# A hybrid decoder layer on one core: 44 output passes in place of 47, every second one added from PSUM by VectorE, and another order at the end

## The reference

```python
def _layer(x, s_gla, s_ssd, s_conv, s_ffn, p):
    xn = _rmsnorm(x, p['n_mix_pre'])
    mix, g_new, h_new, c_new = _mixer(xn, s_gla, s_ssd, s_conv, p)
    x = x + _rmsnorm(mix, p['n_mix_post'])
    xn = _rmsnorm(x, p['n_ffn_pre'])
    f, f_new = _conv_ffn(xn, s_ffn, p)
    x = x + _rmsnorm(f, p['n_ffn_post'])
...
def _conv_ffn(xn, s_ffn, p):
    u = xn @ p['ffn_w_in']                      # 2048 -> 2 * 5632
    u, buf = _causal_dwconv(u, s_ffn, p['ffn_conv_w'], p['ffn_conv_b'])
    a, b = jnp.split(u, 2, axis=-1)
    return (jax.nn.silu(a) * b) @ p['ffn_w_out'], buf.astype(xn.dtype)   # 5632 -> 2048
```

## Time and profile before

| | |
|---|---|
| median of 3 runs | 2520.68 us (2518.03 to 2522.0) |
| the profiled execution | 2520.21 us, its span 2518.4 us |
| granted TensorE clock, mean | 0.989 |
| TensorE busy | 2445.3 us, 97% |
| VectorE busy | 1875.0 us, 74% |
| ScalarE busy | 1099.0 us, 44% |
| GpSimd busy | 424.9 us, 17% |
| passes of the down-projection | 1958.86 to 2453.02 us |
| tail | 2462.32 us to the end |

### The profile page before, as it was taken

The page is one execution under the profiler, slowest core; times in us unless marked ns, Lnnn a source line. Parts: engine busy times, 40 slices in busy tenths (PEclk is TensorE's granted clock), DMA queues, the critical chain, the costliest instruction groups (busy, mean ns, idle before and its releaser), DMA issues.

```text
span 2518.4 us, 48870 instructions
## 1 busy us (share of the span) xinstructions
PE 2445.3 (97%) x20078; PEld 2411.2 (96%) x20078; DVE 1875.0 (74%) x2820; ACT 1099.0 (44%) x1702; POOL 424.9 (17%) x246
## 2 busy tenths in 40 slices
PE   7999999999999999989999999999999999999996
PEld 7999999999999999989999999999999999999995
DVE  6544545766146258898888898888899897798887
ACT  5332222433224235444444444444444665555542
POOL 3333222433223344000000000000000000000005
PEclk9999999999999999999999999999999999999997
DMA  5222227622273424233333333333333465656663
GB/s 177 89 82 90 81 93 265 235 75 68 94 270 119 154 71 152 87 101 104 107 107 109 114 113 104 107 107 109 113 114 120 139 162 159 170 143 174 167 175 110
DMA packets 103246, 322.96 MB, mean 128 GB/s; under 512 B 11120, under 2 KB 15856, under 8 KB 102144
## 3 DMA queue, kind: packets, MB, share of 16 engines
q1 hardware_dynamic: 58336, 211.84, 26.6%
q10 hardware_dynamic: 39232, 88.60, 9.9%
q0 software_dynamic: 5472, 19.61, 4.5%
HBM read 255.77 MB, written 44.62 MB: 119 GB/s over the span
## 4 chain that ended last, share of the span: by engine, by line
PE 64%; issue 15%; DVE 10%; POOL 4%; DMA 4%; ACT 2%; POOLq 0%; ACTq 0%; DVEq 0%; SPq 0%
PE psum_proj L1412 10%; PE psum_proj L1913 7%; PE psum_proj L1915 7%; PE psum_proj L1914 7%; PE psum_work L1913 7%; PE psum_work L1915 7%; PE psum_work L1914 7%; PE psum_proj L1414 5%; POOL w_lo L609 4%; DMA raw<-in_weights_dram 3%; PE psum_work L1412 1%; DVE w_lo L2567 1%; PE psum_work L1414 1%; DVE arena L2833 1%; DVE arena L2483 1%
## 5 line engine op out<-in xcount | busy, mean ns | idle before, releaser
L1412 PE MATMUL psum_proj<-x_hi,w_hi 128*128 128x288 f32 (+2 forms) x1696 | 510.7, 301 | 15.0 <-DVE x_lo L2064 12.9
L1412 PE MATMUL psum_proj<-x_lo,w_hi 128*128 128x288 f32 (+2 forms) x1696 | 500.9, 295 | 0.0
L1414 PE MATMUL psum_proj<-x_hi,w_lo 128*128 128x288 f32 (+2 forms) x1696 | 500.6, 295 | 0.0
L609 POOL TENSOR_TENSOR w_lo<-raw,w_hi 128x1024 fp32r<-128x1024 f32 x128 | 321.6, 2515 | 619.1 <-ACT w_hi L705 619.1
L705 ACT ACTIVATE w_hi<-raw 128x1024 fp32r<-128x1024 f32 x138 | 145.2, 1056 | 484.8 <-PE psum_proj L1414 406.5
L1412 PEld LDWEIGHTS psum_proj<-x_hi,w_hi 128*128 128x128 f32 x1696 | 320.6, 189 | 22.3 <-issue 15.5
L1412 PEld LDWEIGHTS psum_proj<-x_lo,w_hi 128*128 128x128 f32 x1696 | 319.8, 189 | 2.7 <-issue 1.9
L1414 PEld LDWEIGHTS psum_proj<-x_hi,w_lo 128*128 128x128 f32 x1696 | 319.5, 188 | 0.0
L666 POOL DMA_DIRECT2D arena<-m_stage x38 | 32.9, 869 | 1425.3 <-ACT m_stage L1241 1424.6
L1913 PE MATMUL psum_proj<-ops_a,w_hi 128*128 128x288 f32 x808 | 241.5, 299 | 15.3 <-DVE arena L2823 9.1
L1915 PE MATMUL psum_proj<-ops_a,w_lo 128*128 128x288 f32 x808 | 240.0, 297 | 0.0
(11 more groups left out here) (463 smaller groups left out, 6836.2 us busy)
## 6 DMA issues: line engine op xcount, KB each, us to landing
raw<-in_weights_dram SPq DMA_DIRECT2D x386, 512.0 KB, 3.6
g_spill<-x_flat ACTq DMA_DIRECT2D x44, 288.0 KB, 2.1
arena<-m_stage POOLq DMA_DIRECT2D x19, 576.0 KB, 5.6
x_flat<-g_spill ACTq DMA_DIRECT2D x17, 576.0 KB, 6.0
arena<-m_stage POOLq DMA_DIRECT2D x19, 432.0 KB, 8.4
spill<-tail ACTq DMA_DIRECT2D x24, 288.0 KB, 2.1
arena<-in_xT_dram SPq DMA_DIRECT2D x4, 1152.0 KB, 10.6
y_spill<-arena ACTq DMA_DIRECT2D x4, 1152.0 KB, 4.9
```

The costliest lines, as they stand in the source:

```text
L609: nc.gpsimd.tensor_tensor(w_lo[:, slot], raw[:, r], w_hi[:, slot].bitcast(F32), ALU.subtract).then_inc(lo_ready, 1)
L1412: nc.tensor.matmul(banks[:, n, 0:b - a], w_hi[:, slot, k], (hi, lo)[part][:, a:b], start=first and part == 0, stop=False)
L1414: mm = nc.tensor.matmul(banks[:, n, 0:b - a], w_lo[:, slot, k], hi[:, a:b], start=False, stop=last)
```

## The change

The windows of the eight pairs are cut anew, so that there are 44 passes, the last ones in the order of pairs 4, 5, 6, 7, 0, 1, 2, 3. Of the 36 passes that are not a pair's first, every second one and the last two are now `BY_VE` (18), which VectorE adds from PSUM into the block sums; the other 18 (`STAGED`) go through `m_stage` and are all added by accumulating transfers. `add_stage` and its place in VectorE's loop go. Pair 2 is combined by GpSimd (a new `combine(2)` in its queue, ahead of its sums of squares), pair 3 by VectorE behind the seventh tail product; pair 1 is the only one combined in the last iteration, and the low part of the third tail block is made ahead of the last pass and not behind it. The tail's tile order follows, buffers of the tail's squares move, and `h` comes back in seven transfers in place of ten.

```diff
-WINDOWS = ((2, 3, 4, 3, 5, 4), (2, 3, 5, 3, 4, 4), (2, 3, 4, 5, 4, 3), (2, 4, 4, 5, 3, 3), (3, 4, 4, 4, 3, 3),
-           (3, 3, 5, 4, 3, 3), (4, 4, 3, 5, 3, 2), (4, 4, 4, 4, 5))
+WINDOWS = ((2, 3, 4, 5, 3, 4), (2, 4, 4, 4, 3, 4), (2, 5, 3, 5, 3, 3), (2, 5, 4, 4, 3, 3), (3, 5, 4, 4, 5),
+           (3, 5, 4, 4, 5), (4, 5, 4, 3, 5), (5, 4, 4, 3, 5))
...
-LAST_TILES = (14, 15) + tuple(range(14))
-
-BY_VE = (len(PASSES) - 2, len(PASSES) - 1)
-STAGED = [p for p, (r, j, first, stop) in enumerate(PASSES) if r and p not in BY_VE]
-BY_DMA, VE_ADDED = STAGED[0::2], STAGED[1::2]
-ADDED_AT = {END_STEP[p] // 2 + 1: p for p in VE_ADDED}
+LAST_TILES = tuple(range(8, 16)) + tuple(range(8))
+
+LATER = [p for p, (r, j, first, stop) in enumerate(PASSES) if r]
+BY_VE = LATER[1:-3:2] + LATER[-2:]
+STAGED = [p for p in LATER if p not in BY_VE]
...
-        combined_at = {min(WUNITS + END_STEP[p] // 2 + 3, ALL_UNITS - 1): (j,) for j, p in enumerate(LAST_PASS)
-                       if p not in BY_VE}
-        combined_at[ALL_UNITS - 1] = (5, 4)
+        combined_at = {min(WUNITS + END_STEP[p] // 2 + 3, ALL_UNITS - 1): j for j, p in enumerate(LAST_PASS)
+                       if p not in BY_VE[-2:]}
...
-            for p in BY_DMA:
+            for p in STAGED:
                 j = PASSES[p][1]
                 for half, (first, stop) in enumerate(((0, M_SPLIT), (M_SPLIT, 7))):
                     pool.wait_ge(*product_out(p, stop - 1))
-                    for before in added_before(p):
-                        pool.wait_ge(*stage_added(before, half))
+                    pool.wait_ge(*added_before(p, half))
                     pool.dma_start(m_of(j, first, stop), m_stage[:, first * HALF:stop * HALF], accum_op=ALU.add)\
                         .then_inc(m_acc[half], 16)
+
+            def combine(j):
+
+                p = LAST_PASS[j]
+                m = m_of(j).rearrange("p (n t) -> p n t", n=7)
+                for half in range(2):
+                    pool.wait_ge(*added(p, half))
+                nc.gpsimd.tensor_tensor(m[:, 2:4], m[:, 2:4], m[:, 0:1].broadcast_to([P, 2, HALF]), ALU.add)\
+                    .then_inc(pool_step, 1)
...
+            combine(2)
...
-                if w > H_FREED and w - H_FREED - 1 < 7:
+                if w > H_FREED:
                     act.wait_ge(units_done, W_UNIT0 + H_FREED + 1)
-                    h_load(w - H_FREED + 2, w - H_FREED + 3)
+                    first = 3 + 2 * (w - H_FREED - 1)
+                    h_load(first, min(first + 2, H_FIRST))
...
-                if added is not None:
-                    add_stage(added, 0)
...
-                if added is not None:
-                    add_stage(added, 1)
...
-            take_pass(BY_VE[1])
-            tail_lows(2)
+            take_pass(BY_VE[-1])
...
                 if e == 6:
-                    combine(6)
+                    combine(3)
                     settle()
+                if e == 11:
+                    ve.wait_ge(pool_step, 5)
```

More of the change, by code:

```diff
@@ L383, in build @@
         H_FIRST = 10
-        fsum, fsum_v = A(2016 * 7, 576), A(0, 576)
-        fsq = [A(2016 * (1 + i), 576) for i in range(3)] + [w_sum_b[:, 0:576]]
+        fsum, fsum_v = A(2016 * 4, 576), A(2016 * 5, 576)
+        fsq = [A(2016 * i, 576) for i in (6, 7, 0)] + [w_sum_b[:, 0:576]]
         const_in = sem("const_in")
@@ L446, in build @@
         block_in.append(sem("block_in4"))
+        pool_step = sem("pool_step")
         m_acc = [sem("m_acc0"), sem("m_acc1")]
@@ L484, in product_out, with added, added_before @@
             if p in BY_VE:
[L485 to L496, removed]
+                return taken, DOWN_TAKEN0 + 7 * BY_VE.index(p) + q + 1
+            return part_out, FT - STD + 7 * (p - sum(i < p for i in BY_VE)) + q + 1
+        def added(p, half):
+            if p in STAGED:
+                return m_acc[half], 16 * (STAGED.index(p) + 1)
+            return product_out(p, M_SPLIT - 1 if half == 0 else 6)
+        def added_before(p, half):
+            return added([i for i in range(p) if PASSES[i][1] == PASSES[p][1]][-1], half)
         HALF_TILES = 4
@@ L505, in build @@
         DOWN_TAKEN0 = UP_TAKEN0 + 6 * (FT - STD)
-        LAST_TAKEN0 = DOWN_TAKEN0 + 2 * len(VE_ADDED) + 7 * len(BY_VE)
+        LAST_TAKEN0 = DOWN_TAKEN0 + 7 * len(BY_VE)
         FREE_MM0 = HALF_TILES
@@ L685, in _ @@
                 square_sum(0, kt)
-            pool.wait_ge(h_back, 160)
+            pool.wait_ge(h_back, 112)
             adds = [kt for kt in range(KT) if kt not in VE_ADDS[0]]
@@ L1239, in take_pass @@
                         if q in (0, M_SPLIT):
-                            act.wait_ge(*(stage_added(STAGED[before - 1], q // M_SPLIT) if before else (op_low, G_OPS0 + 1)))
+                            act.wait_ge(*((m_acc[q // M_SPLIT], 16 * before) if before else (op_low, G_OPS0 + 1)))
                     nc.scalar.activation(to, bank(7 * p + q), ACT.Copy).then_inc(part_out, 1)
@@ L2816, in take_pass @@
                 j = PASSES[p][1]
-                for before in added_before(p):
-                    for half in range(2):
-                        ve.wait_ge(*stage_added(before, half))
+                for half in range(2):
+                    ve.wait_ge(*added_before(p, half))
                 for q in range(7):
@@ L2823, in take_pass @@
                     tt_op(m, bank(7 * p + q), m, ALU.add).then_inc(taken, 1)
-            def add_stage(p, half):
-                j = PASSES[p][1]
-                first, stop = ((0, M_SPLIT), (M_SPLIT, 7))[half]
-                for before in added_before(p):
-                    ve.wait_ge(*stage_added(before, half))
-                ve.wait_ge(*product_out(p, stop - 1))
-                m = m_of(j, first, stop)
-                tt_op(m, m_stage[:, first * HALF:stop * HALF], m, ALU.add).then_inc(taken, 1)
             def combine(j):
@@ L2838, in combine @@
                 m = m_of(j).rearrange("p (n t) -> p n t", n=7)
-                if p in BY_VE:
-                    ve.wait_ge(*product_out(p, 6))
-                else:
-                    for half in range(2):
-                        ve.wait_ge(*stage_added(p, half))
+                for half in range(2):
+                    ve.wait_ge(*added(p, half))
                 own(tt_op(m[:, 2:4], m[:, 2:4], m[:, 0:1].broadcast_to([P, 2, HALF]), ALU.add))
@@ L2942, in _ @@
                     sum_lows(w + 1)
-                added = ADDED_AT.get(w - WUNITS)
-                if added is not None:
-                    add_stage(added, 0)
                 for low_kp, half in g_low_at.get(w, ()):
@@ L2971, in _ @@
                     tail_lows(w - ALL_UNITS + 2)
-                for j in combined_at.get(w, ()):
-                    if w >= ALL_UNITS - 1:
-                        settle()
-                    combine(j)
+                if w in combined_at:
+                    combine(combined_at[w])
+                if w == ALL_UNITS - 1:
+                    tail_lows(2)
                 if w == TAIL_FREED + 3:
                     g_tail_lows()
-            take_pass(BY_VE[1])
-            tail_lows(2)
+            take_pass(BY_VE[-1])
             def take_last(e):
```

10 lines of the change are left out of this document (9 added, 1 removed).

## The result

The changed kernel takes **2524.89 us** (median of 13 runs, 2521.57 to 2529.75) against 2519.97 us for the kernel before (13 runs on the same chip): ratio 1.0021, 95% interval [1.0011, 1.0030]. It is slower, by 0.1 to 0.3%, where 2513.3 us and "faster" were forecast; the time lies just outside the range. The execution that was profiled took 2526.61 us, span 2524.8.

What follows compares the result with a forecast made beforehand. TensorE was taken to be held by late PSUM copies of ScalarE in the passes and by VectorE's queue at their end. Terms -4.2 - 6 + 8 - 5.2 = -7.4 from 2520.7 gave 2513.3 us, range 2503 to 2524.

Steps and rivals of the forecast that it cites:

- No wait for a full stage, -4.2: Passes, unit 69: staged passes no longer follow another within 8 us, so ScalarE's wait for a full stage goes, -4.2 us.
- The remaining losses of the passes, -6: Passes: of the remaining 17 us of losses, VectorE adding every second pass wins 6 us; bounds -17 and +8.
- its bound of +8: Passes: the remaining 17 us of losses grow by half as much again if VectorE's lag is worse, +8 us.
- the two terms: Passes: the full-stage wait goes, -4.2 us, and the remaining losses shrink, -6 us.
- Two operand pairs with too little room, +8: Units 17 and 69: TensorE waits for late low parts of pairs 6 and 20, +8 us together; bounds 0 and +12.
- The end, -5.2: End of the passes: VectorE's queue before the tail gets shorter, -5.2 us with slow clock; bounds -2 to -7.
- rival (a): Whole kernel: pass adds and late operand pairs cost what stage and end give, +2.6 or -1.4 us; chance 0.18.
- Rival (b): Passes: VectorE held at the finished pass while weights are late, pass-add stalls, +12.6 us, 2533; chance 0.13.
- Rival (d): End: the VectorE-GpSimd port costs 3.6 instead of 1, VectorE arrives late; end -2, whole -4.2, 2516.5 us; chance 0.12.

Runs made afterwards that it cites:

- nearly empty transfers: The changed kernel with accumulating transfers that carry 32 columns instead of 1152 and 864, their order and number kept: 2508.4 us, ratio 0.9960.
- the assignment alone: The kernel before with every second later pass added by VectorE from PSUM, old windows and old end kept: 2518.5 us, ratio 0.9992.
- the version of 2516.8 us: The changed kernel with low parts of pairs 6 and 20 earlier, smaller `h` loads, GpSimd's combine held until the last pass is added: ratio 0.9984.

## Why the prediction was wrong, step by step

- **No wait for a full stage, -4.2: right in its place.** ScalarE no longer waits for `m_stage`'s transfer (6.9 us in four before), and unit 69's loss has another cause now.
- **The remaining losses of the passes, -6: this is the step that failed.** The kernel before lost 20.9 us behind the first two units, 16.7 without the stage wait; the changed one 26.8, 16.8 without the operand pairs. The term was 0. Unit by unit, the gain was there and was given back. Behind ScalarE's copies the kernel before lost 16.0 us in nine stalls (unit 69 left out), the changed one 10.6 in six (units 35, 39, 56, 62, 65, 79): -5.4. Where VectorE adds passes, and where TensorE starts a unit behind VectorE's last low part, the changed kernel loses 5.5 (1.9 in unit 25, 2.1 in 29 and 33, 1.5 in 78), the kernel before 0.5. The prediction had named the cost of a held VectorE (its bound of +8), but took the gain of the shorter queue to outweigh it by 6; they were about equal.

  For units 29, 33 and 78, and for ScalarE's copies, the order of events is read from the timelines; no run changes these queues by themselves. In units 29 and 33, where the pass ends mid-unit, VectorE waits 2.4 and 2.9 us for weights, then adds the pass (2.6 us), and only then makes the low parts with which TensorE starts units 30 and 34, 0.61 and 0.72 us late. With nearly empty transfers units 25, 29, 33 and 78 lose nothing, and the copies' units 4.6 in place of 10.6, so what starts most of these stalls are the late transfers. For the stalls that stayed, the working has ScalarE late because it waits for weights itself. In all six its last wait, of 1.5 to 4.6 us, was for VectorE's weight sums (in the kernel before, in six of nine). In units 33 to 35 the late load held VectorE first, and its pass add went ahead of the sums (VectorE, ScalarE, TensorE):

```profile
2160.52 0.69 DVE L2554 TENSOR_TENSOR w_sum_b<-raw 128x512 f32<-128x512 f32 x1 [2.94 <-DMA raw<-in_weights_dram]
...
2166.69 1.06 ACT L1098 ACTIVATE w_third<-w_sum_b 128x1024 fp32r<-128x1024 f32 x1 [5.33 <-DVE w_sum_b L2568]
...
2171.00 1.06 ACT L1098 ACTIVATE w_hi<-tail 128x1024 fp32r<-128x1024 f32 x1 [2.52 <-DVE tail L2568]
2171.97 0.69 ACT L1259 ACTIVATE m_stage<-psum_work 128x288 f32<-128x288 f32 x2
...
2172.41 0.40 PE L1932 MATMUL psum_work<-ops_a,w_third 128*128 128x288 f32 x1 [1.22 <-ACT m_stage L1259]
```

  The working also left out another thing that is late: VectorE waits for the operands' transfers from `g_spill` in its own queue, ahead of a pass that ends with the unit. With a staged pass the copies stand in another queue than this wait, though ScalarE can meet it at second hand, as in unit 70 of the assignment alone. This part was tested, and in the changed kernel it is the 1.9 us of unit 25. There the accumulating transfers go out at 2096.65 and 2097.75, the operand's load at 2099.97, and the changed kernel's chain of waits and its VectorE timeline go on:

```profile
2099.97 10.44 DMA x_flat<-g_spill
```

```profile
2110.43 0.76 DVE L2801 TENSOR_TENSOR x_flat<-x_flat 128x576 f32<-128x576 f32 x1 [6.82 <-DMA x_flat<-g_spill]
...
2112.51 0.45 DVE L2841 TENSOR_TENSOR arena<-psum_proj,arena 128x288 f32<-128x288 f32 x1
```

  TensorE waits 1.67 us at 2113.02 for that add. The experiment that moves the sums behind the add shows this cause, on a version in which units 20 and 25 lose 6.0 us by it; the changed kernel itself could get back some 1.9 by it (an estimate, from unit 25's loss). The assignment alone won 2.8 us in the passes where the two terms promised 10.2, and 6.4 of its losses lie in two units behind such waits.
- **Two operand pairs with too little room, +8: right in kind and place, somewhat small.** 10.0 us; taking the lateness away gave 6.1 back. The two TensorE waits were 2.45 and 4.08 us where 2.5 and 2.5 were worked out. That stalls under 2 us cost only themselves did not always hold: in units 78 and 79 stalls of 1.37 and 1.49 us lie 2 us apart, slow matmuls follow (granted clock 0.58 from 2433.2 to 2436), and the two units lose 4.9.
- **The end, -5.2: three fifths of it came.** The pause shrank by 3.2. Of the terms, the contention of VectorE and GpSimd was mis-sized: 1.0 was taken, the stretch of VectorE's operations is 1.25 + 0.65 + 1.23 = 3.1. And two things stood in no term: the second block of the tail's weights landed late (ScalarE's wait of 6.20), and VectorE's add of the last pass but one waited 1.66 us, until 2451.88, for an accumulating transfer into the same sums. On the old windows the same edit lengthens the pause (9.3 to 10.7, 8.6 to 10.7), on the new ones it shortens it (7.0 to 6.1): 2.3 of the 3.2 came with the windows and the assignment, not with the new end.

Put the measured terms in: -4.2 + 0 + 10.0 - 3.2 = +2.6, the 1.5 of the first two units 4.1, and the later start and longer tail 2.3: the span's 6.4. This is rival (a), "the time is only moved", in its mechanism. That its sum is +2.6 as well is luck: it had 12 for the operand pairs and -5.2 for the end, where 10.0 and -3.2 were measured. The medians' difference of 4.9 us lies at the border of what was called the same. Rival (b) in its full size didn't occur: TensorE's waits for the pass adds sum to 1.9 us in the passes. Its mechanism, VectorE's held queue while weights are late, is in the 5.5 us above and in unit 35. Rival (d)'s cause, over 2 us of stretch, did occur, beside (a).

One thing stays open: why the staged scheme of the kernel before suffers so much more from the new windows (+15.1 us in the passes) than the new assignment does (+9.3). The traces show a part of it: with the new windows on the old scheme ScalarE waits for a full stage three times, 8.5 us, in units 61, 64 and 67, which lose 2.0, 2.1 and 2.1 us; the changed kernel has no such wait. Units 25 and 39 weren't tested by a run.

## What to carry to other kernels

When work that frees the bottleneck's buffers moves to another engine, look in that engine's queue for every wait for a transfer ahead of it, not only at its load: here two of these waits cost 6 us in one version, until the operand sums stood behind the pass add. Look also at what stands behind the moved work: the low parts and sums that the other engines wait for. When a schedule gets fewer, longer passes, compute for every operand the units between its making and its first use; here two pairs with two units instead of four cost 10.0 us, more than the 7.4 forecast for the whole change. And what VectorE and GpSimd do from SBUF at the same time didn't add up here: look for a place for GpSimd's work where VectorE reads PSUM or stands still.

## What the runs showed of the hardware

- **VectorE and GpSimd on SBUF.** Beside each other, operations with SBUF operands alone took: VectorE 0.95 instead of 0.46, 1.99 instead of 0.75, 2.46 instead of 1.21; GpSimd 1.67 instead of 0.81 and 2.41 instead of 1.41. VectorE's adds from PSUM did not suffer, nor did GpSimd beside them. The timeline of the version of 2516.8 us, where both run at once:

```profile
2461.20 0.80 POOL L680 TENSOR_TENSOR arena<-arena 128x288 f32<-128x288 f32 x1
2461.42 0.46 DVE L2988 TENSOR_TENSOR arena<-psum_proj,arena 128x288 f32<-128x288 f32 x1 [0.91 <-PE psum_proj L1938]
...
2463.71 1.42 POOL L685 TENSOR_TENSOR arena<-arena 128x576 f32<-128x576 f32 x1
2464.03 2.18 DVE L2865 TENSOR_TENSOR w_lo<-raw,w_hi 128x1024 fp32r<-128x1024 f32 x1
```

  0.46 and 0.80 for the add from PSUM, as alone; 2.18 for the low part from SBUF, 2.5 us later.
- **Accumulating transfers within SBUF slowed what loaded beside them.** A 576 KB operand load took 10.44 us two microseconds behind a pair of them and 4.5 (median) when they carried 16 KB. That their bytes are the cause was shown; by which resource, was not.
